# Two reorderings in a one-core streaming encoder step: the first unit's products in three passes, and the x updates of the output units ahead of two sums

## The chip, the cores and the metric

The kernel runs on one NeuronCore of a Trainium2 chip. The metric is the device time of one execution in microseconds (us); lower is better. Engines are TensorE (PE in the profile, with its weight loads as PEld), VectorE (DVE), ScalarE (ACT), GpSimd (POOL) and SyncE (SP), which here only issues DMAs.

## What is computed

A two-layer encoder with 512 prompt tokens and 32 sample tokens, taken together as 544 columns. Around each mixer stand two half-step FFNs, so there are four FFNs; the first is the first thing that runs:

```python
for layer in range(DEPTH):                       # DEPTH = 2
    x = x + 0.5 * swiglu(rms_norm(x, ffn1_norm[layer]), ffn1_w_in[layer], ffn1_w_out[layer])
    h = rms_norm(x, mix_norm[layer])
    ...                                          # attention + HGRN2 (even), gated DeltaNet (odd)
    x = x + o
    x = x + 0.5 * swiglu(rms_norm(x, ffn2_norm[layer]), ffn2_w_in[layer], ffn2_w_out[layer])
y = rms_norm(x, final_norm)
```

`swiglu(h, w_in, w_out)` is `(silu(gate) * up) @ w_out` with `gate, up = split(h @ w_in, 2)`. D_MODEL is 1024 and D_FF 2816, all in float32.

## The kernel before

**Layout.** `x` lies in SBUF as eight tiles of 128 features by 544 tokens. Each product in near-float32 precision is made of three products of a reduced type: the operand and the weight are each split into a high part (`xh`, `wh`: a ScalarE copy that rounds) and a low part (`xl`, `wl`: a VectorE subtraction), and TensorE sums high by high, high by low (of x) and low (of the weight) by high. The 544 tokens go in two matmuls, of 288 and 256 columns; such two matmuls are called a pair here. Two PSUM banks hold one output tile of 128 by 544.

**Norm.** The first product of an FFN takes x times gain, without the norm's factor. Beside it ScalarE squares the tiles (`sq`, L678), GpSimd adds the squares up in `ssq` (`feed_pool`, L686 to L696), TensorE sums over the partitions (`stats_pe`, L698), ScalarE takes the square root (`stats_act`, L705), VectorE the reciprocal (`stats_dve`, L709). The factor is multiplied in behind the product.

**Start.** SyncE issues the loads of `x_sample`, the first half of x's features (`xnat`, counted in `in_loaded`), the first unit's weights (`raw[0]`), the second half of x (`in2_loaded`), some small vectors, and then a stream of weights that waits for buffers. ScalarE issues `ident` and seven rows of gains, eight DMAs in `vec_loaded`. `load_pe` (L3217) waits for all eight, turns the gain rows into columns in bank 6 (L3221), then transposes the eight tiles of x through three slots of PSUM banks (L3233, L3234). `load_dve` (L3250) copies each into `x` and follows it with the low part of the tile before (`feed_dve`, L680); with tile 4 it makes the low part of the first weights (`split_lo`, L641, 128 by 2048). ScalarE makes the high part of a tile and its square in turn (`feed_act`, L670), with the high part of the weights (`split_hi`, L633) ahead of tile 4.

**First unit.** `ffn_whole_pe` (L786) waits for the low part of the weights, and for each of two output tiles c runs over the eight tiles k of x with three pairs each (`mm3`, L652). For the first FFN (`u.f == 0`) the statistics come behind c = 1, and then `late_pe` (L3237): it waits for the square root and transposes further small vectors (L3244 to L3248). Then comes the second unit (L782).

**Order.** Each engine has one program order written out by hand, and waits for others by counters (semaphores).

**Output units.** In each FFN, groups of two "seven" units (inputs' products, L852) alternate with one "mid" unit, 32 in all, eight for each FFN, which multiplies four tiles of the hidden layer by `w_out` and adds the result to x. A mid unit has four blocks on TensorE (`ffn_mid_pe`, L861), of twelve pairs each, which use two PSUM slots in turn: block m may start once the x update of block m - 2 is done. VectorE runs beside it (`ffn_mid_dve`, L1221): for the next seven unit v it makes four sums of weight blocks (`weight_sum_dve`, L991) and the low parts of what ScalarE has rounded (`op_split_lo`, L769), the low parts of the hidden layer (`hidden_lo`, L912) and the four x updates (`x_update`, L1170), of which the last stands in the unit behind.

Of the kernel before, what the change touches and what calls it, by code (L numbers as in the profile page):

```python
# [24 lines left out]
ACT = mybir.ActivationFunctionType  # L25
# [4 lines left out]
P = 128  # L30
D = 1024
KT = D // P
SEQ = 512
DEC = 32
T = SEQ + DEC
TOKENS = (slice(0, 288), slice(288, T))
PCOLS = (slice(224, 512), slice(0, T - 288))
# [115 lines left out]
def build(nc, ctx, io):  # L153
# [14 lines left out]
    def again(first, count):  # L168

        return Later(first.sem, first.credit + count)  # L170
# [374 lines left out]
    sm_packed = again(lam_exp, 1)  # L545
    tail_psum = again(an_wide, 4)
    tail_copied = again(an_hi, 4)
    tail_stored = again(in_loaded, 32)

    y_scaled = again(an_inv, 3)  # L550
    y_psum = again(an_psum, 1)
# [62 lines left out]
    def entry(op):  # L614
# [2 lines left out]
        flat = lambda w: w[e // 4][:].rearrange("p k n -> p (k n)")[:, (e % 4) * KH * P:(e % 4 + 1) * KH * P]  # L617
        block = lambda w: flat(w).rearrange("p (k n) -> p k n", n=P)
        return block(wh), block(wl)
    VECS, LATE = 8, 9  # L620

    def late_vectors(sp):
        sp.dma_start(rows_conv[0:4, :], io["conv_w"][0]).then_inc(late_loaded.sem, 16)
# [17 lines left out]
    def split_lo(dve, u, slot, kt=KT):  # L641

        dve.wait_ge(hi_done.sem, hi_done.at(u + 1))
        nc.vector.tensor_tensor(wl[slot][:, 0:kt, :], raw[slot][:, 0:kt, :], wh[slot][:, 0:kt, :].bitcast(F32),  # L644
                                ALU.subtract).then_inc(lo_done.sem, 1)
# [17 lines left out]
    def gain_of(n, m):  # L663
        return gain(n, m) if isinstance(m, int) else gain_at(n, m)

    def tile(buf, m):

        return buf[:, m, :] if isinstance(m, int) else buf[:, ds(m, 1), :].rearrange("p a t -> p (a t)")

    def feed_act(act, n, m, par, products=True):  # L670

        act.wait_ge(x_ready.sem, x_ready.at(8 * n + m + 1))
        set_apart(act)
        if products:
            nc.scalar.activation(tile(xh, m), tile(x, m), ACT.Copy, scale=gain_of(n, m)).then_inc(xh_ready.sem, 1)
        act.wait_ge(ssq_done.sem, ssq_done.at(8 * n + m - 1))
        set_apart(act)
        nc.scalar.activation(sq[par][:], tile(x, m), ACT.Square).then_inc(sq_ready.sem, 1)  # L678
# [35 lines left out]
    def slot_free(pe, n, slot):  # L714

        pe.wait_ge(x_ready.sem, x_ready.at(8 * n + 5 + slot))
# [52 lines left out]
    def op_split_lo(dve, u, i):  # L769
        op, nk = u.op + i, block_nk(u, i)  # L770
        hi, lo = entry(op)
        dve.wait_ge(op_hi.sem, op_hi.at(op + 1))
        nc.vector.tensor_tensor(lo[:, 0:nk, :], op_source(u, i), hi[:, 0:nk, :].bitcast(F32), ALU.subtract).then_inc(op_lo.sem, 1)  # L773

    def block3(pe_out, op, nk, rh, rl, rk, first, last):
# [7 lines left out]
                                           start=first and k == 0 and a == 0, stop=last and k == nk - 1 and a == 2)  # L783
        return ins

    def ffn_whole_pe(pe, u, n):  # L786
        c0 = U_FFN[u.f]
        pe.wait_ge(lo_done.sem, lo_done.at(c0 + 1))
        for c in range(2):
            if u.f:  # L790
                slot_free(pe, n, c)
            for k in range(KT):
                if c == 0:
                    pe.wait_ge(xl_ready.sem, xl_ready.at(8 * n + k + 1))
                last = mm3(c, 0, k, c, xh, xl, k, k == 0, k == KT - 1)
            last.then_inc((gate_psum if c == 0 else unit_done).sem, 1)
            if c == (1 if u.f == 0 else 0):
                stats_pe(pe, n)
                if u.f == 0:
                    late_pe(pe)  # L800

    def ffn_plain_pe(pe, u, n):
        f, j = u.f, u.pair
# [366 lines left out]
    def x_update(dve, u, c):  # L1170

        m = 4 * u.pair + c
        dve.wait_ge(op_used.sem, op_used.at(u.op + c + 1))
        if u.part:
            dve.wait_ge(x_part.sem, x_part.at(part_updates(u, m - 7)))
        nc.vector.scalar_tensor_tensor(out=two(x[:, m, :]), in0=halves(2 + c % 2), scalar=0.5, in1=two(x[:, m, :]),  # L1176
                                       op0=ALU.mult, op1=ALU.add).then_inc(x_part.sem, 1)
# [43 lines left out]
    def ffn_mid_dve(dve, u):  # L1221
        before, v = ffns[u.f][u.at - 1], ffns[u.f][u.at + 1]
        tail_dve(dve, before)
        weight_sum_dve(dve, v, 0)
        op_split_lo(dve, v, 0)
        weight_sum_dve(dve, v, 1)
        op_split_lo(dve, v, 1)
        weight_sum_dve(dve, v, 2)
        weight_sum_dve(dve, v, 3)
        hidden_lo(dve, before, 0, 1)  # L1230
        x_update(dve, u, 0)
        op_split_lo(dve, v, 2)
        hidden_lo(dve, before, 1, 2)
        op_split_lo(dve, v, 3)
        x_update(dve, u, 1)
        op_split_lo(dve, v, 4)
        op_split_lo(dve, v, 5)
        x_update(dve, u, 2)
        op_split_lo(dve, v, 6)
# [1976 lines left out]

    def load_pe(pe):  # L3217

        pe.wait_ge(vec_loaded.sem, vec_loaded.at(16 * VECS))
        for m in range(KT):  # L3220
            ins = nc.tensor.transpose(ps[:, 6, 7 * m:7 * m + 7], rows_gain[:, m * P:(m + 1) * P], ident[0:7, 0:7])  # L3221
        ins.then_inc(cols_psum.sem, 1)
        for m in range(KT):
            if m == 0:
                pe.wait_ge(in_loaded.sem, in_loaded.at(32))
            if m == 2:
                pe.wait_ge(cols_ready.sem, cols_ready.at(1))
            if m == KT // 2:
                pe.wait_ge(in2_loaded.sem, in2_loaded.at(16))
            pe.wait_ge(x_ready.sem, x_ready.at(m - 2))  # L3230
            s = 1 + m % 3
            for b in range(NB):
                nc.tensor.transpose(ps[:, 2 * s, b * P:(b + 1) * P], xnat[:, b, m * P:(m + 1) * P], ident[:])  # L3233
            nc.tensor.transpose(ps[:, 2 * s + 1, 0:DEC], xnat_dec[:, m * P:(m + 1) * P],  # L3234
                                ident[0:DEC, 0:DEC]).then_inc(xt_done.sem, 1)

    def late_pe(pe):  # L3237

        pe.wait_ge(late_loaded.sem, late_loaded.at(16 * LATE))
        pe.wait_ge(consts_set.sem, consts_set.at(1))  # L3240
        pe.wait_ge(rms_ready.sem, rms_ready.at(1))
        pe.wait_ge(cols_ready.sem, cols_ready.at(1))
        for m in range(24):
            nc.tensor.transpose(ps[:, 6, 7 * (KT + m):7 * (KT + m) + 7], rows_conv[:, m * P:(m + 1) * P], ident[0:7, 0:7])  # L3244
        for m in range(4):
            nc.tensor.transpose(ps[:, 6, LB + 2 * m:LB + 2 * m + 2], rows_lb[:, m * P:(m + 1) * P], ident[0:2, 0:2])
        nc.tensor.transpose(ps[:, 6, G3:G3 + 3], rows_g3[:], ident[0:3, 0:3]).then_inc(cols_psum.sem, 1)
        nc.tensor.matmul(ps[:, 7, 0:272], ones[0:1, :], row_lam[:], start=True, stop=True).then_inc(lam_psum.sem, 1)  # L3248

    def load_dve(dve):  # L3250
        dve.wait_ge(cols_psum.sem, cols_psum.at(1))
        nc.vector.tensor_copy(cols[:, 0:7 * KT], ps[:, 6, 0:7 * KT]).then_inc(cols_ready.sem, 1)
        nc.vector.tensor_copy(pick[0:32, :], ident[0:32, 0:16])
        nc.vector.tensor_copy(pick[32:48, :], ident[32:48, 32:48])
        for m in range(KT):
            dve.wait_ge(xt_done.sem, xt_done.at(m + 1))
            s = 1 + m % 3
            nc.vector.tensor_copy(x[:, m, 0:SEQ], ps[:, 2 * s, :])
            nc.vector.tensor_copy(x[:, m, SEQ:T], ps[:, 2 * s + 1, 0:DEC]).then_inc(x_ready.sem, 1)
            if m == KT // 2:  # L3260
                split_lo(dve, 0, 0)
            if m:
                if m == 1:
                    dve.wait_ge(cols_ready.sem, cols_ready.at(1))
                feed_dve(dve, 0, m - 1)
        feed_dve(dve, 0, KT - 1)

    def late_dve(dve):
        dve.wait_ge(cols_psum.sem, cols_psum.at(2))
# [98 lines left out]
    @block.scalar  # L3368
    def _(act):
        for s in (hi_done, tap0):  # L3370
            s.credit_by(act)

        act.dma_start(ident[:], io["c_ident"]).then_inc(vec_loaded.sem, 16)
        for l in range(2):
            for r, name in enumerate(("ffn1_norm", "mix_norm", "ffn2_norm")):
                act.dma_start(rows_gain[3 * l + r:3 * l + r + 1, :], io[name][l:l + 1, :]).then_inc(vec_loaded.sem, 16)
        act.dma_start(rows_gain[6:7, :], io["final_norm"].rearrange("(a n) -> a n", a=1)).then_inc(vec_loaded.sem, 16)
        act.wait_ge(cols_ready.sem, cols_ready.at(1))
        for m in range(KT):
            if m == KT // 2:  # L3380
                split_hi(act, 0, 0)
            feed_act(act, 0, m, m % 2)
        ffn_act(act, 0, 0, U_EVEN)
        even_proj_act(act, 1)
        hgrn_act(act)
        out_act(act, U_EVEN + 14, PLAIN_PARTS, 2, False)
        ffn_act(act, 1, 2, U_FFN[2])
        ffn_act(act, 2, 3, U_ODD)
        odd_act(act, 4)
        out_act(act, U_ODD + 16, PLAIN_PARTS, 5, False, True)  # L3390
        ffn_act(act, 3, 5)
        output_act(act, 6)
# [77 lines left out]
```

## Time and profile before

| | us |
|---|---|
| three runs | 2361.01, 2366.35, 2360.02 |
| their median | 2361.01 |
| the profiled execution | 2359.82 |
| its span | 2358.0 |

| engine | busy, us | share of the span |
|---|---|---|
| PE | 2311.9 | 98% |
| PEld | 2255.4 | 96% |
| DVE | 1646.2 | 70% |
| ACT | 1063.1 | 45% |
| POOL | 298.9 | 13% |

The span is what the profiler saw from first to last instruction; the device time of the same execution is 1.8 us more. Times in views are us from the span's start, those of single instructions may be in ns. Matmuls are pipelined, so two that follow each other overlap in the list; how far apart they start tells the pace. The profile's share of granted clock is 1 at the upper of TensorE's two levels (2.4 GHz) and 0.5 at the lower (1.2 GHz).

### The profile page before, as it was taken

How to read it: one execution, taken by the hardware profiler on the slowest of the kernel's cores; microseconds unless marked ns; L12 is line 12 of the kernel's file. 1: busy time of each engine (PE TensorE's matmuls, PEld its weight loads, DVE VectorE, ACT ScalarE, POOL GpSimd, SP SyncE). 2: the span in 40 equal slices, each digit the busy share in tenths (PEclk: the TensorE clock that was granted, in tenths of full speed). 3: DMA queues.
4: the chain of work that ended last, by engine and by line, in shares of the span. 5: the costliest groups of instructions: out<-in, count | busy, mean ns of one | idle time of the engine just before them, and what ended most of it. 6: DMA issues, size and time to landing. Idle time of an engine off the chain costs nothing.

```text
span 2358.0 us, 44517 instructions
## 1 busy us (share of the span) xinstructions
PE 2311.9 (98%) x18296; PEld 2255.4 (96%) x18296; DVE 1646.2 (70%) x2689; ACT 1063.1 (45%) x1951; POOL 298.9 (13%) x252
## 2 busy tenths in 40 slices
PE   7999999999999999999999999999999999999998
PEld 6999999988989999999999999999999899999998
DVE  6876776656575967776976676788655657877674
ACT  4544444233324544444544444455344544544443
POOL 2100002000051100001200000243033432100001
PEclk9999999999999999999999999999999999999999
DMA  3322323322202222322223222322200002232222
GB/s 118 103 90 90 99 94 116 98 85 80 70 10 90 90 90 91 108 90 90 90 90 106 92 90 90 101 72 90 77 27 1 10 28 90 90 107 91 90 91 73
DMA packets 174905, 194.70 MB, mean 83 GB/s; under 512 B 4810, under 2 KB 155726, under 8 KB 174697
## 3 DMA queue, kind: packets, MB, share of 16 engines
q1 hardware_dynamic: 161902, 181.64, 23.6%
q10 hardware_dynamic: 12162, 8.11, 1.2%
q8 instruction: 147, 2.41, 0.4%
q0 software_dynamic: 640, 2.10, 0.3%
q14 instruction: 54, 0.44, 0.1%
HBM read 185.73 MB, written 6.10 MB: 81 GB/s over the span
## 4 chain that ended last, share of the span: by engine, by line
PE 91%; DVE 5%; issue 1%; ACT 1%; POOL 0%; DMA 0%; ACTq 0%; DVEq 0%
PE ps L852 31%; PE ps L782 28%; PE ps L659 19%; PE ps L3061 2%; PE ps L3046 1%; PE ps L3192 1%; DVE wl L644 1%; PE ps L3034 1%; PE ps L1631 1%; PE ps L2099 0%; PE ps L2196 0%; DVE hl L916 0%; PE ps L1320 0%; DVE wl L773 0%; PE ps L3080 0%
## 5 line engine op out<-in xcount | busy, mean ns | idle before, releaser
L852 PE MATMUL ps<-bop,wh 128*128 128x272 f32 x4032 | 764.0, 289 | 0.0
L852 PEld LDWEIGHTS ps<-bop,wh 128*128 128x128 f32 x4032 | 633.6, 188 | 0.1
L852 PE MATMUL ps<-bop,wl 128*128 128x272 f32 x2016 | 583.6, 289 | 0.0
L773 DVE TENSOR_TENSOR wl<-raw,wh 128x512 fp32r<-128x512 f32 (+1 forms) x456 | 318.2, 710 | 279.3 <-ACT wh L767 274.8
L852 PEld LDWEIGHTS ps<-bop,wl 128*128 128x128 f32 x2016 | 379.1, 188 | 0.0
L767 ACT ACTIVATE wh<-raw 128x512 fp32r<-128x512 f32 (+1 forms) x456 | 264.8, 610 | 247.2 <-PE ps L782 209.8
L782 PE MATMUL ps<-hh,wh 128*128 128x288 f32 (+1 forms) x1408 | 290.4, 287 | 5.5 <-DVE x L1176 5.5
L782 PE MATMUL ps<-hl,wh 128*128 128x288 f32 (+1 forms) x1408 | 289.6, 287 | 0.0
L782 PE MATMUL ps<-hh,wl 128*128 128x288 f32 (+1 forms) x1408 | 288.7, 286 | 0.0
L659 PE MATMUL ps<-xh,wh 128*128 128x288 f32 x1088 | 232.7, 295 | 3.9 <-DVE wl L644 2.8
L782 PEld LDWEIGHTS ps<-hh,wh 128*128 128x128 f32 x1408 | 215.0, 188 | 11.4 <-issue 11.4
L659 PE MATMUL ps<-xl,wh 128*128 128x288 f32 x1088 | 224.5, 287 | 0.0
L659 PE MATMUL ps<-xh,wl 128*128 128x288 f32 x1088 | 223.7, 287 | 0.0
L782 PEld LDWEIGHTS ps<-hh,wl 128*128 128x128 f32 x1408 | 215.2, 188 | 0.0
L782 PEld LDWEIGHTS ps<-hl,wh 128*128 128x128 f32 x1408 | 214.7, 188 | 0.0
L767 ACT ACTIVATE wh<-wsum 128x512 fp32r<-128x512 f32 x256 | 159.6, 627 | 112.6 <-DVE wsum L998 86.6
L773 DVE TENSOR_TENSOR wl<-wsum,wh 128x512 fp32r<-128x512 f32 x256 | 175.1, 684 | 17.4 <-ACT wh L767 13.7
L659 PEld LDWEIGHTS ps<-xh,wh 128*128 128x128 f32 x1088 | 166.6, 189 | 16.2 <-issue 7.4
L692 POOL COPY ssq<-sq 128x544 f32<-128x544 f32 x7 | 5.2, 741 | 1307.4 <-ACT sq L678 1307.4
L659 PEld LDWEIGHTS ps<-xh,wl 128*128 128x128 f32 x1088 | 166.7, 188 | 0.0
L659 PEld LDWEIGHTS ps<-xl,wh 128*128 128x128 f32 x1088 | 166.4, 188 | 0.0
L644 DVE TENSOR_TENSOR wl<-raw,wh 128x2048 fp32r<-128x2048 f32 x41 | 94.5, 2304 | 38.7 <-ACT wh L639 38.7
(475 smaller groups left out, 3692.4 us busy)
## 6 DMA issues: line engine op xcount, KB each, us to landing
raw<-ffn_w_in SPq DMA_DIRECT2D x88, 1024.0 KB, 5.1
raw<-ffn_w_out SPq DMA_DIRECT2D x32, 1024.0 KB, 5.0
raw<-odd_w_in SPq DMA_DIRECT2D x16, 1024.0 KB, 5.8
raw<-even_w_in SPq DMA_DIRECT2D x14, 1024.0 KB, 5.0
raw<-ffn_w_out SPq DMA_DIRECT2D x16, 768.0 KB, 4.2
raw<-even_w_out SPq DMA_DIRECT2D x4, 1024.0 KB, 5.0
raw<-odd_w_out SPq DMA_DIRECT2D x4, 1024.0 KB, 5.2
xnat<-x_prompt SPq DMA_DIRECT2D x2, 1024.0 KB, 12.1
```

What stands on the lines that cost most here:

```text
L644: nc.vector.tensor_tensor(wl[slot][:, 0:kt, :], raw[slot][:, 0:kt, :], wh[slot][:, 0:kt, :].bitcast(F32), ALU.subtract).then_inc(lo_done.s ...
L659: ins = nc.tensor.matmul(ps[:, 2 * pe_out + b, PCOLS[b]], w, r[:, rk, TOKENS[b]], start=first and a == 0, stop=last and a == 2)
L692: nc.gpsimd.tensor_copy(ssq[:], sq[0][:]).then_inc(ssq_done.sem, 1)
L767: nc.scalar.activation(entry(op)[0][:, 0:block_nk(u, i), :], op_source(u, i), ACT.Copy).then_inc(op_hi.sem, 1)
L773: nc.vector.tensor_tensor(lo[:, 0:nk, :], op_source(u, i), hi[:, 0:nk, :].bitcast(F32), ALU.subtract).then_inc(op_lo.sem, 1)
L782: ins = nc.tensor.matmul(ps[:, 2 * pe_out + b, PCOLS[b]], w[:, k, :], r[:, rk + k, TOKENS[b]], start=first and k == 0 and a == 0, stop=las ...
L852: ins = nc.tensor.matmul(ps[:, bank, 0:TH], w[:, k, :], bop[:, r, k, :], start=i in S_OPEN and k == 0 and a == 0, stop=k == KH - 1 and a = ...
L1631: ins = nc.tensor.matmul(ps[:, 4 + m, 0:width(b)], att[64 * m:64 * m + 64, h, b * P:(b + 1) * P], att[64 * m:64 * m + 64, 4 + h, 0:width(b ...
L3034: ins = nc.tensor.transpose(bank(g, 2, n, n)[:, h, :], dX[g][0:n, h, 0:n], ident[0:n, 0:n])
L3046: ins = nc.tensor.matmul(bank(g, 0, n, n)[:, h, :], strict[0:n, h, 0:n], dX[g][0:n, h, 0:n], start=True, stop=True)
L3061: ins = nc.tensor.matmul(bank(g, 0, n, n)[:, h, :], dU[g][0:n, h, 0:n], dZ[g][0:n, h, 0:n], start=True, stop=True)
L3192: ins = nc.tensor.matmul(ps[:, 2 * (2 * q + c) + b, PCOLS[b]], w, r[:, k, TOKENS[b]], start=k == 0 and a == 0, stop=k == KT - 1 and a == 2)
```

## The change

In the first unit:

- TensorE runs all high by high products over both output tiles (for each tile of x, both c), then all high by low, then low by high, c = 0 and then c = 1. The passes wait for `hi_done`, `xl_ready` and `lo_done` in turn. The statistics stand behind c = 0 of the third pass, `late_pe` behind c = 1.
- `load_pe` starts on x when `ident` (now counted in `in_loaded`) and the first half of x are in, and transposes the gains after two tiles, into bank 0. The slots of the tiles are shifted by one.
- VectorE copies two tiles, then the gains, then for each tile m its copy and the low part of tile m - 2; the low part of the first weights comes last.
- ScalarE loads the gains of both layers with one DMA for each norm, runs a Square on a spare column ahead of its first wait, makes the high part of the weights ahead of tile 3, and squares only tiles 0 and 1 between the copies; the squares of tiles 2 to 7 come behind all copies.

In the output units (`ffn_mid_dve`) the x update of block 0 moves ahead of the third and fourth sum.

```diff
@@ feed_act
-    def feed_act(act, n, m, par, products=True):
+    def feed_act(act, n, m, par, products=True, squares=True):
...
+        if not squares:
+            return
         act.wait_ge(ssq_done.sem, ssq_done.at(8 * n + m - 1))
@@ first unit
+    def first_whole_pe(pe):
+        w_hi, w_lo = wh[0], wl[0]
+
+        def product(c, k, w, r, first, last):
+            for b in range(2):
+                ins = nc.tensor.matmul(ps[:, 2 * c + b, PCOLS[b]], w[:, k, c * P:(c + 1) * P], r[:, k, TOKENS[b]],
+                                       start=first, stop=last)
+            return ins
+
+        pe.wait_ge(hi_done.sem, hi_done.at(1))
+        for k in range(KT):
+            pe.wait_ge(xh_ready.sem, xh_ready.at(k + 1))
+            for c in range(2):
+                if k == 0 and c == 1:
+                    pe.wait_ge(x_ready.sem, x_ready.at(6))
+                product(c, k, w_hi, xh, k == 0, False)
+        for k in range(KT):
+            pe.wait_ge(xl_ready.sem, xl_ready.at(k + 1))
+            for c in range(2):
+                product(c, k, w_hi, xl, False, False)
+        pe.wait_ge(lo_done.sem, lo_done.at(1))
+        for c in range(2):
+            for k in range(KT):
+                last = product(c, k, w_lo, xh, False, k == KT - 1)
+            last.then_inc((gate_psum if c == 0 else unit_done).sem, 1)
+            if c == 0:
+                stats_pe(pe, 0)
+        late_pe(pe)
@@ ffn_mid_dve
         op_split_lo(dve, v, 1)
+        x_update(dve, u, 0)
         weight_sum_dve(dve, v, 2)
         weight_sum_dve(dve, v, 3)
         hidden_lo(dve, before, 0, 1)
-        x_update(dve, u, 0)
@@ load_pe
-        pe.wait_ge(vec_loaded.sem, vec_loaded.at(16 * VECS))
+        pe.wait_ge(in_loaded.sem, in_loaded.at(48))
         for m in range(KT):
-            ins = nc.tensor.transpose(ps[:, 6, 7 * m:7 * m + 7], rows_gain[:, m * P:(m + 1) * P], ident[0:7, 0:7])
-        ins.then_inc(cols_psum.sem, 1)
-        for m in range(KT):
-            if m == 0:
-                pe.wait_ge(in_loaded.sem, in_loaded.at(32))
             if m == 2:
-                pe.wait_ge(cols_ready.sem, cols_ready.at(1))
+                pe.wait_ge(vec_loaded.sem, vec_loaded.at(16 * VECS))
+                for g in range(KT):
+                    ins = nc.tensor.transpose(ps[:, 0, 7 * g:7 * g + 7], rows_gain[:, g * P:(g + 1) * P], ident[0:7, 0:7])
+                ins.then_inc(cols_psum.sem, 1)
...
-            s = 1 + m % 3
+            s = 1 + (m + 1) % 3
@@ load_dve
+        turned(0)
+        turned(1)
         dve.wait_ge(cols_psum.sem, cols_psum.at(1))
...
+        dve.wait_ge(cols_ready.sem, cols_ready.at(1))
+        for m in range(2, KT):
+            turned(m)
+            feed_dve(dve, 0, m - 2)
+        feed_dve(dve, 0, KT - 2)
         feed_dve(dve, 0, KT - 1)
+        split_lo(dve, 0, 0)
@@ scalar
-        act.dma_start(ident[:], io["c_ident"]).then_inc(vec_loaded.sem, 16)
-        for l in range(2):
-            for r, name in enumerate(("ffn1_norm", "mix_norm", "ffn2_norm")):
-                act.dma_start(rows_gain[3 * l + r:3 * l + r + 1, :], io[name][l:l + 1, :]).then_inc(vec_loaded.sem, 16)
+        act.dma_start(ident[:], io["c_ident"]).then_inc(in_loaded.sem, 16)
+        for r, name in enumerate(("ffn1_norm", "mix_norm", "ffn2_norm")):
+            act.dma_start(rows_gain[r:r + 4:3, :], io[name]).then_inc(vec_loaded.sem, 16)
...
+        act.wait_ge(consts_set.sem, consts_set.at(1))
+        nc.scalar.activation(lamv[:, 7:8], eps[:, 0:1], ACT.Square)
         act.wait_ge(cols_ready.sem, cols_ready.at(1))
         for m in range(KT):
-            if m == KT // 2:
+            if m == 3:
                 split_hi(act, 0, 0)
-            feed_act(act, 0, m, m % 2)
+            feed_act(act, 0, m, m % 2, squares=m < 2)
+        for m in range(2, KT):
+            feed_act(act, 0, m, m % 2, products=False)
```

## Rows read from the trace of the kernel before

**Rows 1.** Waits of TensorE: us in total, times, longest us.
```profile
PE ps L3221 <- DMA rows_gain<-final_norm: 8.3, 1, 8.3
PE ps L782 <- DVE x L1176: 5.5, 4, 1.4
PE ps L659 <- DVE wl L644: 3.5, 2, 2.8
```

**Rows 2.** Chain of waits, 0 to 80 us: start us, us, what.
```profile
30.76 6.99 PE ps L659 x54
...
42.16 37.48 PE ps L782 x288
```

**Rows 3.** Timeline of TensorE, start: start us, us, engine, line, instruction [idle before].
```profile
9.26 1.11 PE L3233 MATMUL ps<-ident,xnat 128*128 128x128 f32 x4
...
14.40 1.11 PE L3233 MATMUL ps<-ident,xnat 128*128 128x128 f32 x4
...
18.42 1.11 PE L3233 MATMUL ps<-ident,xnat 128*128 128x128 f32 x4
...
22.58 0.82 PE L659 MATMUL ps<-xh,wh 128*128 128x288 f32 x2 [2.81 <-DVE wl L644]
...
25.46 0.48 PE L659 MATMUL ps<-xh,wh 128*128 128x288 f32 x2
...
37.59 1.08 PE L702 MATMUL ps<-ssq,ones 128*128 128x288 f32 x4
39.67 1.61 PE L3244 MATMUL ps<-ident,rows_conv 7*128 7x7 f32 x24 [1.01 <-ACT ssq L707]
...
42.09 0.52 PE L782 MATMUL ps<-xh,wh 128*128 128x288 f32 x2
```

**Rows 4.** Issue of x's second half, and its time to landing.
```profile
2.20 0.61 SPq L3354 DMA_DIRECT2D xnat<-x_prompt  x1
...
DMA to landing us min/median/max: 12.1/12.1/12.1
```

**Rows 5.** Timeline of GpSimd: three adds of squares, at the start and the end.
```profile
21.26 2.47 POOL L696 TENSOR_TENSOR ssq<-ssq,sq 128x544 f32<-128x544 f32 x1 [0.89 <-ACT sq L678]
...
28.50 1.62 POOL L696 TENSOR_TENSOR ssq<-ssq,sq 128x544 f32<-128x544 f32 x1 [0.18 <-POOL ssq L696]
...
2336.00 1.36 POOL L696 TENSOR_TENSOR ssq<-ssq,sq 128x544 f32<-128x544 f32 x1 [2.60 <-ACT sq L678]
```

**Rows 6.** Timeline of VectorE and ScalarE at the start.
```profile
19.83 2.69 DVE L644 TENSOR_TENSOR wl<-raw,wh 128x2048 fp32r<-128x2048 f32 x1 [1.47 <-ACT wh L639]
...
26.33 0.77 DVE L682 SCALAR_TENSOR_TENSOR xl<-x,cols,xh 128x544 fp32r<-128x544 f32 x1
...
27.72 2.98 DVE L682 SCALAR_TENSOR_TENSOR xl<-x,cols,xh 128x544 fp32r<-128x544 f32 x2
27.91 0.75 ACT L675 ACTIVATE xh<-x,cols 128x544 fp32r<-128x544 f32 x1
...
30.62 3.65 DVE L773 TENSOR_TENSOR wl<-raw,wh 128x512 fp32r<-128x512 f32 x4
```

**Rows 7.** Busy time of each engine in one us; the third number from the end is the granted clock.
```profile
43.00:44.00 1.00, 1.00 (x6) 1.00 (x6) 0.97 (x3) 0.20 (x1) 0.00 (x0) 0.50 0.00 0
```

**Rows 8.** Timelines of the first output unit, and of the second.
```profile
105.61 0.68 DVE L1004 TENSOR_TENSOR wsum<-raw,wsum 128x512 f32<-128x512 f32 x1
...
107.45 0.72 DVE L1176 SCALAR_TENSOR_TENSOR x<-ps,x 128x544 f32<-128x544 f32 x1
...
108.31 0.49 PE L782 MATMUL ps<-hh,wh 128*128 128x288 f32 x2 [1.37 <-DVE x L1176]
...
109.92 0.72 DVE L1176 SCALAR_TENSOR_TENSOR x<-ps,x 128x544 f32<-128x544 f32 x1
...
138.28 0.41 PE L782 MATMUL ps<-hh,wl 128*128 128x288 f32 x2
...
138.96 0.68 DVE L1004 TENSOR_TENSOR wsum<-raw,wsum 128x512 f32<-128x512 f32 x1
...
139.67 1.24 ACT L767 ACTIVATE wh<-wsum 128x512 fp32r<-128x512 f32 x2 [0.15 <-DVE wsum L1004]
```

More of the change, by code:

```diff
@@ L547, in build @@
     tail_copied = again(an_hi, 4)
-    tail_stored = again(in_loaded, 32)
+    tail_stored = again(in_loaded, 48)
     y_scaled = again(an_inv, 3)
@@ L619, in entry @@
         return block(wh), block(wl)
-    VECS, LATE = 8, 9
+    VECS, LATE = 4, 9
     def late_vectors(sp):
@@ L784, in block3 @@
         return ins
+    def first_whole_pe(pe):
[24 more added lines that the diff above has]
+        late_pe(pe)
     def ffn_whole_pe(pe, u, n):
+        if u.f == 0:
+            first_whole_pe(pe)
+            return
         c0 = U_FFN[u.f]
@@ L789, in ffn_whole_pe @@
         for c in range(2):
-            if u.f:
-                slot_free(pe, n, c)
+            slot_free(pe, n, c)
             for k in range(KT):
@@ L796, in ffn_whole_pe @@
             last.then_inc((gate_psum if c == 0 else unit_done).sem, 1)
-            if c == (1 if u.f == 0 else 0):
+            if c == 0:
                 stats_pe(pe, n)
-                if u.f == 0:
-                    late_pe(pe)
     def ffn_plain_pe(pe, u, n):
@@ L3250, in load_dve, with turned @@
     def load_dve(dve):
+        def turned(m):
+            dve.wait_ge(xt_done.sem, xt_done.at(m + 1))
+            s = 1 + (m + 1) % 3
+            nc.vector.tensor_copy(x[:, m, 0:SEQ], ps[:, 2 * s, :])
+            nc.vector.tensor_copy(x[:, m, SEQ:T], ps[:, 2 * s + 1, 0:DEC]).then_inc(x_ready.sem, 1)
+        turned(0)
+        turned(1)
         dve.wait_ge(cols_psum.sem, cols_psum.at(1))
-        nc.vector.tensor_copy(cols[:, 0:7 * KT], ps[:, 6, 0:7 * KT]).then_inc(cols_ready.sem, 1)
+        nc.vector.tensor_copy(cols[:, 0:7 * KT], ps[:, 0, 0:7 * KT]).then_inc(cols_ready.sem, 1)
         nc.vector.tensor_copy(pick[0:32, :], ident[0:32, 0:16])
         nc.vector.tensor_copy(pick[32:48, :], ident[32:48, 32:48])
[L3255 to L3259, printed above, removed]
-            if m == KT // 2:
[L3261 to L3265, printed above, removed]
+        dve.wait_ge(cols_ready.sem, cols_ready.at(1))
[3 more added lines that the diff above has]
+        feed_dve(dve, 0, KT - 2)
         feed_dve(dve, 0, KT - 1)
+        split_lo(dve, 0, 0)
     def late_dve(dve):
@@ L3371, in _ @@
             s.credit_by(act)
-        act.dma_start(ident[:], io["c_ident"]).then_inc(vec_loaded.sem, 16)
-        for l in range(2):
-            for r, name in enumerate(("ffn1_norm", "mix_norm", "ffn2_norm")):
-                act.dma_start(rows_gain[3 * l + r:3 * l + r + 1, :], io[name][l:l + 1, :]).then_inc(vec_loaded.sem, 16)
+        act.dma_start(ident[:], io["c_ident"]).then_inc(in_loaded.sem, 16)
+        for r, name in enumerate(("ffn1_norm", "mix_norm", "ffn2_norm")):
+            act.dma_start(rows_gain[r:r + 4:3, :], io[name]).then_inc(vec_loaded.sem, 16)
         act.dma_start(rows_gain[6:7, :], io["final_norm"].rearrange("(a n) -> a n", a=1)).then_inc(vec_loaded.sem, 16)
+        act.wait_ge(consts_set.sem, consts_set.at(1))
+        nc.scalar.activation(lamv[:, 7:8], eps[:, 0:1], ACT.Square)
         act.wait_ge(cols_ready.sem, cols_ready.at(1))
         for m in range(KT):
-            if m == KT // 2:
+            if m == 3:
                 split_hi(act, 0, 0)
-            feed_act(act, 0, m, m % 2)
+            feed_act(act, 0, m, m % 2, squares=m < 2)
+        for m in range(2, KT):
+            feed_act(act, 0, m, m % 2, products=False)
         ffn_act(act, 0, 0, U_EVEN)
```

## The prediction

> **What bounds the kernel now.** I read the list of TensorE's waits first. It is short: 8.3 us for the first loads, 5.5 us in four waits for an x update of VectorE, 3.5 us for the low part of the first weights [rows 1]. The chain of waits then says that from 42.16 us on TensorE runs 288 products without a gap up to 79.64 [rows 2]. So the kernel is bound by the count of TensorE's products, and only what lets TensorE begin earlier, or takes one of those waits away, can move the end. The change works at two such places: the first 42 us, and the four waits of 1.4 us.
>
> In the timeline of the start the reader is to see four stretches [rows 3]: eight tiles of x transposed from 9.26 to 19.7 (1.28 us a tile), 2.8 us of waiting for the low weights, 48 pairs of products from 22.58 to 37.59, and then statistics, a wait for the square root and 29 tiny transposes until 42.09, where the second unit begins. I price TensorE's work from here: 27 pairs from 30.76 [rows 2] to 37.59 [rows 3] are 0.25 us a pair at the upper clock level; the first six pairs took 2.9 us (22.58 to 25.46), 0.45 us for most.
>
> **The change part by part, at the start.**
>
> Loads. The second half of x is issued at 2.20 us and lands 12.1 us later, at 14.3 [rows 4]; the fifth tile was transposed at 14.40 [rows 3], so in the kernel before that landing was just met. The change doesn't touch SyncE's queue. ScalarE issues three gain loads in place of six; whatever that saves, and the earlier start of the first tiles (they no longer stand behind the gain loads, at least 8.3 us before), ends at the same landing. I take no gain from it. The cover is thin on the other side: two tiles, eight gain transposes (about 1 us) and two more tiles are 6.1 us, so the first half of x must be in by 8.2 us. The trace shows only that it was in by 9.26. If it lands then, TensorE ends its transposes 1.1 us late; I keep this for the range. So TensorE is through with its transposes at 14.35 + 4 x 1.29 = 19.5 us.
>
> First products. They now need only the high parts of weights and x, and begin at 19.55 in place of 22.58. Nothing of before shows dense products right behind transposes. The transposes did not bring the quick pace before: the six pairs behind them were slow. I take the same 2.9 us for the first six pairs. Of the 48 pairs 40 stand ahead of the statistics: 2.9 + 34 x 0.25 = 11.4, so TensorE comes to the statistics at 30.95.
>
> VectorE. It now turns two tiles before the gains, and the 2.7 us split of the low weights [rows 6] goes behind all tiles. A copy and a low part take 1.39 us a tile (26.33 to 27.72) [rows 6]; the last tile is transposed at 19.5, VectorE is then busy with the fifth low part until 20.2, copies the last tile until 20.9, and is done with the low parts at 23.1 to 24 and with the weights at about 26. The third pass wants them at 28.9. So both waits, of 2.8 us and 1.1 us, go at no price; what is queued behind the split is only the second unit. The reload of that weight buffer starts some 3.5 us later than before, but is read only behind the first square root; were this cover gone, it would cost 1 us for 1 us.
>
> ScalarE and GpSimd. Six of eight squares go behind all copies. This is what is late next. The last copy ends at 20.9 + 0.75 = 21.65 [rows 6], the third square at 22.3, and GpSimd then has six adds left, where before only three lay behind 26.7. The trace has three prices [rows 5]: 1.36 us where VectorE leaves it alone, 1.62 beside low parts, 2.47 where the split of 128x2048 lies beside it; 0.18 between two. I place them: one beside the last low parts (1.62), one beside the split (2.47), three alone (1.36 each, VectorE has nothing to do from 26 to 30.4), one beside the next unit's splits (1.62). That is 9.8 + 0.9 = 10.7 us, and the sum of squares is ready at 33.0. TensorE has waited 2 us for it.
>
> Statistics and late transposes. Statistics 1.0 us (37.59 to 38.68 before) until 34.0. The other half of the third pass, eight pairs, 2.0 us, lies beside the square root, which had cost TensorE 1.0 us of waiting. Late transposes 2.4 us as before (39.67 to 42.09). The second unit begins at 34.0 + 2.0 + 2.4 = 38.4 in place of 42.09: **3.7 us**. VectorE's reciprocal comes earlier by 4.7 us (square root ready at 34.7 in place of 39.4), so its chain into the next units moves by more than TensorE's, and the gap-free run of rows 2 stays one.
>
> Bounds of this term: six adds alone are 9.1 us, ready at 31.4, TensorE 5.3 us earlier; six adds at 2.47 are 15.7 us, ready at 38.0, TensorE 1.3 us later than before. I take the placement above, since each price there has a row with the same neighbour.
>
> Clock. From 43 to 44 us the granted clock is 0.50, the lower level of 1.2 GHz [rows 7]; it holds for about seven pairs at 0.45 in place of 0.25, 1.4 us. It fell after TensorE had done, since 38.68, only a wait and small transposes, 3.4 us. In the changed kernel the longest such stretches are the wait of 2 us and, 3 us of dense work later, the 2.4 us of transposes. I take it that the clock doesn't fall: **1.4 us**; the ends are 0 and 1.4, and something like the loss of 1.4 could come in the 2 us wait instead.
>
> **The change part by part, output units.** There are 32 (eight for each FFN). In the first of each FFN TensorE's third product block waits for the x update of block 0: that update starts at 107.45, TensorE at 108.31 after 1.37 us [rows 8]. Two sums of 0.6 us and one low part stand ahead of it. Moved, it starts at 105.61, where the first of the sums stood, and ends at 106.3, before TensorE asks (106.94). But the fourth block waits for the update of block 1, and that one keeps its place: it starts at 109.92 and ends at 110.6, as all that stands ahead of it is only reordered, and VectorE has no idle time there. TensorE, now through with the third block at 110.0, waits 0.7 us for it. So of 1.37 us 0.67 stays: x 4 = **2.7 us**. The ends are 0 (VectorE shifted by as much) and 5.5.
>
> In the other 28 units the update comes to stand where the sum now starts, at 138.96 in the unit of 135.53; the last pair of the block that it needs starts at 138.28 and takes 0.41 [rows 8]. So it waits for nothing, with 0.3 us in hand. The sums come 0.65 us later; ScalarE's copies of them are taken up by the unit after, several us away. I cost it at nothing; what it costs without that cover is the slower rival.
>
> **Sum.** 3.7 + 1.4 + 2.7 = 7.8 us. The profiled execution took 2359.8 us (span 2358.0 and 1.8 around it), 1.2 less than the median of the runs, 2361.0; the four times have their middle at about 2360.3. I go from there: 2352.5 us.
>
> **The rivals.**
>
> The clock falls all the same (in the wait ahead of the statistics or behind the late transposes): 6.4 us, 2353.9. For: such a wait is new. Against: neither stretch is as long as the one that preceded the fall.
>
> GpSimd starves. Here six adds meet low parts, the long split and the next four splits. For: the add beside the long split took 2.47 us, and most of the excess over 1.36 is the 1.24 us in which that split still ran [rows 5, 6]. If every such VectorE instruction stops GpSimd outright, the adds' 9.1 us and VectorE's 0.7 + 2.3 + 4 x 0.6 go one after the other: 14.5 us, ready at 36.8, the second unit at 42.2, nothing won at the start. Left is 2.7: 2357.6. Against: beside short instructions it was VectorE that was stretched (two low parts in 2.98 us, four splits in 3.65 [rows 6]), GpSimd only from 1.36 to 1.62. The Trainium skill (GPSIMD Engine Reference, 1. Specifications) says that GpSimd shares its SBUF interfaces with VectorE, with contention for VectorE instructions with two SBUF inputs; by that rule, taken as exclusion, this rival is the outcome, and the trace bears it out only in part.
>
> GpSimd is hardly stretched, sum ready at 31.4 to 31.9: 5.0 + 1.4 + 2.7 = 9.1, 2351.2. For: VectorE is idle through most of it.
>
> Slower. In the 28 regular output units the moved update has 0.3 us in hand. If VectorE waits there, or the delay of 0.65 us of two sums reaches TensorE through ScalarE's copies, it is paid 28 times: up to 18 us, less the 7.8 of the rest, 2370.7. It decides from the point at which the sums' copies have under 0.65 us in hand before their products. Against: ScalarE has copied both sums by 140.9 [rows 8], and their products stand in the unit after, which begins 12 us behind the start of this one at 135.53.
>
> The waits for x updates aren't what holds the output units (the place of VectorE as a whole is): 5.1 us, 2355.2.
>
> **How the numbers follow.** Forecast 0.46, clock falls 0.21, starved 0.11, hardly stretched 0.13, update worth nothing 0.05, slower 0.03, first half of x late (2353.5) within the forecast; 0.01 for the rest. Range: from the free GpSimd with some room, 2350.0, to the starved one, 2357.6. About 0.3% (7 us, below 2353.9 where the runs' median is 2361.0) is what a measurement of this kernel can tell from no change. The forecast lies on the near side of it by 1.4 us only: 0.8 of it counts as faster, a third of the clock rival, all of the free GpSimd: 0.55. Slower 0.03. Within 0.42.
>
> **What would show it.** Right: first products at 19.5 without a wait for the low weights; a TensorE wait of about 2 us for the sum of squares near 31 to 33; none for the square root; second unit at 38.4; no 0.50 in the clock near 40; in each FFN's first output unit no wait at the third block and one of 0.7 us at the fourth. Wrong: the sum of squares ready before 31 or after 35, products at the slow pace for longer than 3 us, a wait at other output units, or a total that moved by more than the start and the four waits did.

## The result, and the profile after

| | before | changed |
|---|---|---|
| median of six runs, us | 2360.2 | 2350.15 |
| lowest to highest, us | 2359.75 to 2366.35 | 2345.86 to 2351.15 |
| profiled execution, us | 2359.82 | 2350.17 |
| its span, us | 2358.0 | 2348.4 |

The medians differ by 10.1 us, where 7.8 were forecast in the sum. The ratio on record is 0.9949 (95% interval 0.9938 to 0.9959); it isn't the quotient of the two medians, which is 0.9957 and lies inside that interval, and the same holds for the ratios of the experiments below. The change is faster by more than 0.3%, but the time stands at the very low end of the range (2350.0 to 2357.6), and by the ratio, 2348.2, just under it. The total hides that both halves of the sum were wrong, in opposite directions.

First the waits of TensorE in the changed kernel (us in total, times, longest us), to set against [rows 1]. The change shifted line numbers: the x update is L1207, the transposes of x are L3262 and L3263, the statistics L704.

```profile
PE ps L3262 <- DMA xnat<-x_prompt: 7.4, 2, 6.3
PE ps L784 <- DVE x L1207: 3.5, 4, 0.9
...
PE ps L704 <- POOL ssq L698: 2.5, 1, 2.5
```

The waits for low weights are gone but for 0.7 us elsewhere; four waits for an x update are left, 0.9 us each in place of 1.4; and there is a new one of 2.5 us for GpSimd's sum of squares. The timeline of TensorE's start, to set against [rows 3]:

```profile
6.26 1.11 PE L3262 MATMUL ps<-ident,xnat 128*128 128x128 f32 x4 [6.26 <-DMA xnat<-x_prompt]
...
13.38 1.12 PE L3262 MATMUL ps<-ident,xnat 128*128 128x128 f32 x4 [1.09 <-DMA xnat<-x_prompt]
...
18.53 6.17 PE L793 MATMUL ps<-xh,wh 128*128 128x288 f32 x32
24.54 4.18 PE L793 MATMUL ps<-xl,wh 128*128 128x288 f32 x32
28.55 2.17 PE L793 MATMUL ps<-xh,wl 128*128 128x288 f32 x16
33.20 2.18 PE L704 MATMUL ps<-ssq,ones 128*128 128x288 f32 x4 [2.47 <-POOL ssq L698]
34.82 3.11 PE L793 MATMUL ps<-xh,wl 128*128 128x288 f32 x16
37.86 1.64 PE L3273 MATMUL ps<-ident,rows_conv 7*128 7x7 f32 x24
...
40.68 0.82 PE L784 MATMUL ps<-xh,wh 128*128 128x288 f32 x2
```

Read the starts. The first products begin at 18.53 (22.58 before), TensorE is at the statistics at 30.6, waits to 33.20, and then takes 1.6 us for the statistics and 3.0 for eight pairs, which took 1.0 and 2.0 in the working of the prediction. The second unit begins at 40.68: 1.4 us earlier, not 3.7. The granted clock shows why. These are stretches of the changed kernel: length, then busy us of PE, PEld, DVE, ACT, POOL with instructions, and the third number from the end is the clock.

```profile
32.50:36.50 4.00, 3.30 (x10) 2.84 (x11) 2.73 (x4) 2.24 (x3) 0.65 (x1) 0.57 0.05 14
36.50:39.50 3.00, 3.00 (x39) 2.85 (x37) 3.00 (x1) 1.47 (x3) 0.00 (x0) 1.00 0.98 333
39.50:47.00 7.50, 7.50 (x37) 6.80 (x36) 7.40 (x12) 4.70 (x7) 3.14 (x2) 0.54 0.01 4
```

TensorE ran at the lower level (1.2 GHz) in two stretches, from 33.0 to 36.5 and from 39.9 to 46.7; before there was one, 3.4 us long (42.7 to 46.1, of which [rows 7] shows one us). By 79.2 us, where the fifth unit begins, only 0.2 us of the start's gain is left (79.47 before, 79.23 after, by the timelines). At the first output unit it is 0.4 us (100.81 and 100.41).

So the 10 us come from the output units. Timelines of the second one (a regular unit), first in the kernel before, with the x update of block 0 on VectorE (L1176), then in the changed kernel:

```profile
135.53 0.42 PE L782 MATMUL ps<-hh,wh 128*128 128x288 f32 x2
...
140.80 0.71 DVE L1176 SCALAR_TENSOR_TENSOR x<-ps,x 128x544 f32<-128x544 f32 x1
...
141.25 0.41 PE L782 MATMUL ps<-hh,wl 128*128 128x288 f32 x2
141.66 0.49 PE L782 MATMUL ps<-hh,wh 128*128 128x288 f32 x2
141.98 0.41 PE L782 MATMUL ps<-hl,wh 128*128 128x288 f32 x2
...
147.70 0.41 PE L852 MATMUL ps<-bop,wh 128*128 128x272 f32 x2
```

```profile
134.63 0.42 PE L784 MATMUL ps<-hh,wh 128*128 128x288 f32 x2
...
140.35 0.41 PE L784 MATMUL ps<-hh,wl 128*128 128x288 f32 x2
140.60 0.40 PE L784 MATMUL ps<-hh,wh 128*128 128x288 f32 x2
...
146.54 0.41 PE L883 MATMUL ps<-bop,wh 128*128 128x272 f32 x2
```

Before, the unit ran from 135.53 to 147.70, 12.17 us; after, from 134.63 to 146.54, 11.91. Between the second and third block the pairs start 0.41 us apart in place of 0.25 (141.25 to 141.66), and the next start comes 0.32 later. The x update ends at 141.51, just as TensorE wants its buffer. That is a stall of a quarter of a microsecond, on none of the lines of the list of TensorE's waits. The traces have it in each of the 28 regular units: all are 12.16 or 12.17 us long before and 11.91 or 11.92 after, 7 us in all. The only sign of it in the lists is in that of the weight loads. These are the waits of TensorE's weight loads in the kernel before, from 120 to 400 us, the stretch with the seven regular units of the first FFN:

```profile
PEld ps L782 <- issue: 1.3, 7, 0.2
```

Seven times 0.2, put down to "issue". In the changed kernel the list of that stretch is empty.

### The profile page after: what moved, and what is told of

Its sections match the earlier page's. It is cut to its first block, busy times and chain, and to the rows that moved or that the text cites. A ratio compares the mean times of both kernels' runs of the same rounds, so it can differ in the third digit from the quotient of the medians.

```text
span 2348.4 us, 44520 instructions
## 1 busy us (share of the span) xinstructions
PE 2307.8 (98%) x18296; PEld 2256.6 (96%) x18296; DVE 1644.0 (70%) x2689; ACT 1063.7 (45%) x1952; POOL 299.8 (13%) x252
## 4 chain that ended last, share of the span: by engine, by line
PE 91%; DVE 6%; issue 1%; ACT 1%; POOL 1%; DMA 0%; DVEq 0%; SPq 0%; ACTq 0%; POOLq 0%
PE ps L883 31%; PE ps L784 27%; PE ps L659 19%; PE ps L3092 2%; PE ps L3077 1%; PE ps L3223 1%; PE ps L3065 1%; DVE wl L775 1%; PE ps L1662 1%; DVE wl L644 0%; POOL ssq L698 0%; DVE hl L947 0%; PE ps L2130 0%; PE ps L2227 0%; PE ps L1351 0%
## 5 line engine op out<-in xcount | busy, mean ns | idle before, releaser
L659 PE MATMUL ps<-xh,wh 128*128 128x288 f32 (+1 forms) x1056 | 225.3, 294 | 0.0
L659 PE MATMUL ps<-xl,wh 128*128 128x288 f32 (+1 forms) x1056 | 217.4, 287 | 0.0
L659 PE MATMUL ps<-xh,wl 128*128 128x288 f32 (+1 forms) x1056 | 216.7, 286 | 0.0
L659 PEld LDWEIGHTS ps<-xh,wh 128*128 128x128 f32 x1056 | 161.1, 188 | 11.7 <-issue 7.4
L659 PEld LDWEIGHTS ps<-xh,wl 128*128 128x128 f32 x1056 | 161.4, 188 | 0.0
L659 PEld LDWEIGHTS ps<-xl,wh 128*128 128x128 f32 x1056 | 161.1, 188 | 0.0
## 6 DMA issues: line engine op xcount, KB each, us to landing
xnat<-x_prompt SPq DMA_DIRECT2D x2, 1024.0 KB, 11.1
```

What stands on the lines that cost most here:

```text
L659: ins = nc.tensor.matmul(ps[:, 2 * pe_out + b, PCOLS[b]], w, r[:, rk, TOKENS[b]], start=first and a == 0, stop=last and a == 2)
```

## The experiments

All times are medians; the kernel before ran beside each of two groups. Its median was 2360.36 beside the kernels with the output units alone, the start alone, the squares between the copies and the statistics behind, and 2359.92 beside the other four. The changed kernel's 2350.15 is that of the first table.

**Which half brought the time.** The output units alone:

```diff
         op_split_lo(dve, v, 1)
+        x_update(dve, u, 0)
         weight_sum_dve(dve, v, 2)
         weight_sum_dve(dve, v, 3)
         hidden_lo(dve, before, 0, 1)
-        x_update(dve, u, 0)
```

> The kernel before with only the x update of block 0 moved ahead of the two sums in the 32 output units. Theory A (from the two traces: each of the 28 regular units was 0.25 us longer before, 12.16 against 11.91 us, since the update of block 0 ended at the moment at which TensorE wanted it; the four first ones 0.5 us): 28 x 0.25 + 4 x 0.5 = 9.0 us, 2351.2 against 2360.2, and 32 output units as long as in the changed kernel. Theory B (my prediction: only the four waits count, the regular units hide the update): 2 to 2.7 us, 2357.5 to 2358.2.

Measured 2351.67 (ratio 0.9957, 0.9945 to 0.9969): 8.7 us, where theory A had 9.0. Theory A holds. The second output unit runs from 135.30 to 147.21, 11.91 us; four waits of 0.9 remain. Next, the start alone:

```diff
@@ the changed kernel, ffn_mid_dve
-        x_update(dve, u, 0)
         weight_sum_dve(dve, v, 2)
         weight_sum_dve(dve, v, 3)
         hidden_lo(dve, before, 0, 1)
+        x_update(dve, u, 0)
```

> The changed kernel with the x update put back behind the sums, so only the start is changed. Theory A (what the start won was given back by a lower clock level, first in the 2.5 us wait for the sum of squares and again behind the late transposes): 0.3 to 1 us faster than before, 2359.2 to 2359.9, with two stretches of granted clock 0.5 before 50 us. Theory B (the start is worth the 5.1 us forecast and the output units the rest): 2355.

Measured 2357.66 in eleven runs, 2355.67 to 2359.59 (ratio 0.9987, 0.9978 to 0.9995): 2.7 us, more than A said and about half of B. The profiled execution was the slowest of them, 2359.59. In it the wait for the sum of squares was 3.2 us, the clock was at 0.50 from 33.1 to 39.9 and again from 43.3 to 46.8, and the first output unit begins when it did before. So the start is worth something between 0.8 and 4.7 us from one execution to the next. That the clock makes this difference is likely, not shown: only one execution has a trace, but the mean granted clock of the whole execution was 0.998 in four of the five quickest and 0.996 or 0.997 in the six others. The two halves add up to 11.4, the changed kernel shows 10.1.

**Is it lateness, or the order?** The update was moved by one place only:

```diff
@@ the kernel before, ffn_mid_dve
         weight_sum_dve(dve, v, 2)
         weight_sum_dve(dve, v, 3)
-        hidden_lo(dve, before, 0, 1)
         x_update(dve, u, 0)
+        hidden_lo(dve, before, 0, 1)
```

> The kernel before with the x update of block 0 moved ahead of one low part of the hidden layer only, so it stays behind both sums: 0.64 us earlier in place of 1.84. Theory A (in the regular units the update missed TensorE's need by 0.25 us, so any move of more than that wins the whole): 9 us, as for the full move, 2351.4; regular units 11.91 us. Theory B (what the regular units won came from the sums being out of the way of it, in proportion to the move): a third, 3 us, 2357.3.

Measured 2350.63 (0.9962, 0.995 to 0.9975), 9.3 us, as much as the full move. Regular units are 11.91 us long (134.97 to 146.88), and the first one of each FFN is 13.02 to 13.04, as with the full move. The waits of TensorE left in this kernel:

```profile
PE ps L782 <- DVE x L1176: 2.9, 4, 0.7
```

In the first output units these are waits at the third block (107.62 us), where the full move left them at the fourth. The move of one place was enough; theory A holds, and the update didn't have to go ahead of the two sums. The regular stall was an update that ended as it was wanted.

**What the first output units still wait for.** On top of the changed kernel, the update of block 1 was moved:

```diff
         op_split_lo(dve, v, 2)
+        x_update(dve, u, 1)
         hidden_lo(dve, before, 1, 2)
         op_split_lo(dve, v, 3)
-        x_update(dve, u, 1)
```

> The changed kernel with the x update of block 1 moved two places ahead as well (before the second low part of the hidden layer and one low part of the weights). If that update is what TensorE waits 0.87 us for in each first output unit: 4 x 0.87 = 3.5 us, 2346.7, with no wait at the fourth block. If VectorE as a whole is late there, the wait goes on to the next product that needs a low part, and the time stays at 2350.2.

Measured 2344.32 (0.9935, 0.9922 to 0.9947), 5.8 us below the changed kernel, where 3.5 were expected. The waits for x updates are gone, and the first output unit lasts 11.92 us in place of 13.04, 4 x 1.12 = 4.5 us. The rest, 1.3 us, is within the spread of its runs (2342.67 to 2348.29); in the profiled execution the start was as much ahead, with the second unit at 39.37 in place of 40.68. That execution was the slowest of the five: from the first to the last of the transposes of L2593, in a later stage, it took 140.1 us (1778.6 to 1918.7) against 136.0 in the changed kernel (1783.4 to 1919.4), 2.4 of these 4.1 us in waits for VectorE that are longer than in the changed kernel. The edit touches nothing there, and the cause is not known. VectorE as a whole wasn't late: nothing took the wait's place.

**What gives the start's gain back.** First the cause of the late sum. GpSimd in the changed kernel:

```profile
21.44 3.82 POOL L698 TENSOR_TENSOR ssq<-ssq,sq 128x544 f32<-128x544 f32 x1 [7.15 <-ACT sq L680]
25.44 1.36 POOL L698 TENSOR_TENSOR ssq<-ssq,sq 128x544 f32<-128x544 f32 x1 [0.18 <-POOL ssq L698]
...
31.58 1.56 POOL L698 TENSOR_TENSOR ssq<-ssq,sq 128x544 f32<-128x544 f32 x1 [0.18 <-POOL ssq L698]
```

The sum is ready at 33.1. VectorE's work beside the long add, and beside the last one:

```profile
19.68 2.17 DVE L684 SCALAR_TENSOR_TENSOR xl<-x,cols,xh 128x544 fp32r<-128x544 f32 x3
21.76 2.28 DVE L644 TENSOR_TENSOR wl<-raw,wh 128x2048 fp32r<-128x2048 f32 x1
31.21 3.68 DVE L775 TENSOR_TENSOR wl<-raw,wh 128x512 fp32r<-128x512 f32 x4 [7.17 <-ACT wh L769]
```

In the next kernel all squares stand between the copies again:

```diff
-            feed_act(act, 0, m, m % 2, squares=m < 2)
-        for m in range(2, KT):
-            feed_act(act, 0, m, m % 2, products=False)
+            feed_act(act, 0, m, m % 2)
```

> The changed kernel with all eight squares between ScalarE's copies, as before; the rest of the change stays. If the late squares are what makes the sum of squares late: GpSimd's sum is ready by 27 us in place of 33.2, TensorE meets the statistics at about 30.7 without a wait, the clock doesn't fall there, the second unit begins at 36 in place of 40.7, and the time is 2345.5, or down to 2343 if the clock doesn't fall behind the late transposes either. If VectorE's low parts, slower beside GpSimd, become the bound of the three passes instead, TensorE waits there and the time stays within 1 us of 2350.2.

Measured 2344.92 (0.9931, 0.992 to 0.9943), 5.2 us below the changed kernel. Its GpSimd and TensorE:

```profile
24.03 1.63 POOL L698 TENSOR_TENSOR ssq<-ssq,sq 128x544 f32<-128x544 f32 x1 [0.18 <-POOL ssq L698]
```

```profile
28.57 2.20 PE L793 MATMUL ps<-xh,wl 128*128 128x288 f32 x16
30.61 1.08 PE L704 MATMUL ps<-ssq,ones 128*128 128x288 f32 x4
...
36.08 0.58 PE L784 MATMUL ps<-xh,wh 128*128 128x288 f32 x2
```

The sum is ready at 25.7, TensorE doesn't wait, the second unit begins at 36.08, and the clock falls once, at 36.4, behind the late transposes. The three passes did not suffer: high by high begins at 18.60, the statistics at 30.61. So it was the late squares, not the passes, that the start paid for. Against the kernel with the output units alone (2351.67) this start is worth 6.8 us.

Next, the clock alone. The wait was filled with products that nothing reads:

```diff
@@ first_whole_pe, ahead of stats_pe
+                for i in range(10):
+                    for b in range(2):
+                        nc.tensor.matmul(ps[:, 6 + b, PCOLS[b]], w_lo[:, i % KT, 0:P], xh[:, i % KT, TOKENS[b]], start=True, stop=True)
```

> The changed kernel with ten pairs of products more (2.5 us; into the banks that the statistics overwrite, so nothing is read of them) in TensorE's wait for the sum of squares. Theory A (the wait without products is what brings the clock down at 33): granted clock 1 at 33 to 36.5, statistics and the last eight pairs at the upper level, 1.6 to 2 us faster than the changed kernel although TensorE does more: 2348.2 to 2348.6, and 2346.8 if the fall behind the late transposes gets shorter too. Theory B (the clock falls in any case, or the fall costs nothing since VectorE's reciprocal is the bound behind it): 2350 or more.

Measured 2347.23 (0.9945, 0.9932 to 0.9957): 2.9 us below the changed kernel, for more work. From 32.5 to 36.5 us:

```profile
32.50:36.50 4.00, 4.00 (x29) 3.66 (x29) 3.73 (x4) 2.30 (x3) 0.75 (x1) 1.00 0.07 9
```

The clock stays up, the second unit begins at 38.87 in place of 40.68, and the later fall is 3.4 us long in place of 6.8. The statistics begin at 33.32, against 33.20, so the added products cost nothing. That is theory A, and between the medians the clock cost the changed kernel 2.9 us. But the fall doesn't follow from the wait with certainty. The same stretch in the kernel with the second update moved, which had the wait of 3.3 us:

```profile
32.50:36.50 4.00, 3.04 (x20) 2.81 (x20) 3.73 (x4) 2.51 (x3) 0.90 (x1) 1.00 0.04 6
```

Here the clock held through a longer wait, and was down from 38.6 to 45.4 instead. These are single executions: where the clock falls differs from one to the next, and I can't say from them how often.

Last, the order of the statistics:

```diff
             last.then_inc((gate_psum if c == 0 else unit_done).sem, 1)
-            if c == 0:
-                stats_pe(pe, 0)
+        stats_pe(pe, 0)
         late_pe(pe)
```

> The changed kernel with the statistics behind both output tiles of the third pass, as before the change. TensorE then comes to the statistics at about 32.7, the sum is ready at 33.2: a wait of 0.5 us in place of 2.5, no fall of the clock at 33; but the wait of 1 us for the square root is back. Second unit at 37.5 in place of 40.7. If the clock fell because of the 2.5 us wait: 2345.5 to 2347. If the order of the statistics is worth what I took it for (1 us) and the clock falls in any case: 2351.

Measured 2348.39 (0.9947, 0.9934 to 0.9959; six runs from 2344.74 to 2353.84). TensorE in the profiled execution, one of the two quickest (2345.11):

```profile
33.53 1.18 PE L704 MATMUL ps<-ssq,ones 128*128 128x288 f32 x4 [1.62 <-POOL ssq L698]
35.72 1.62 PE L3272 MATMUL ps<-ident,rows_conv 7*128 7x7 f32 x24 [1.01 <-ACT ssq L709]
...
38.17 0.82 PE L784 MATMUL ps<-xh,wh 128*128 128x288 f32 x2
```

Part of this was expected: no fall at 33, the wait for the square root back, the second unit at 38.17, 0.7 later than expected. The wait for the sum was 1.6 us, not 0.5: the first pass was 0.8 us shorter here (18.51 to 23.71), and the sum was ready 0.3 later. The median lies between the two theories. The mean granted clock was 0.997 or 0.998 in the three quicker runs and 0.996 in the three slower ones, so the clock differs here too, and with this spread the runs don't decide how much this order alone is worth.

**Together.** Squares between the copies and the second update moved, both on the changed kernel:

```diff
-            feed_act(act, 0, m, m % 2, squares=m < 2)
-        for m in range(2, KT):
-            feed_act(act, 0, m, m % 2, products=False)
+            feed_act(act, 0, m, m % 2)
...
         op_split_lo(dve, v, 2)
+        x_update(dve, u, 1)
         hidden_lo(dve, before, 1, 2)
         op_split_lo(dve, v, 3)
-        x_update(dve, u, 1)
```

> The changed kernel with the squares between the copies (as in e3_squares_between) and the x update of block 1 two places ahead (as in e6_second_update). The two places don't touch each other: 2344.9 less 3.5, 2341.4. If one eats up the other: not below 2343.

Measured 2340.64 (0.9915, 0.9901 to 0.9928): 19.3 us below the kernel before, 9.5 below the changed one, and the gains add up (4.3 us on top of the squares alone). Of all kernels here it is the fastest.

## Why the prediction was right or wrong

**The 28 regular output units, costed at nothing: wrong, 7.0 us, the largest error.** The step that failed is "So it waits for nothing, with 0.3 us in hand" and, resting on it, "I cost it at nothing". The step asked whether VectorE would have to wait in the new place. It didn't ask whether TensorE was waiting in the old one, and it was, for 0.25 us in each unit. The numbers were there: the update started at 140.80 and takes 0.7, TensorE wants it 24 pairs after 135.53, at 141.5. My 0.25 us a pair, times 48, gives a unit of 12.0 by the same working, and 12.17 was measured. I read the list of waits as complete, and it is not: the list shows a pair as 0.41 us long where the next begins after 0.25, so a start that is 0.16 late leaves no idle time to be seen.

**The four first units: mechanism right, size off.** The third block's wait went, a wait at the fourth came. The wait measured 0.87 us, not 0.7, and the unit got 0.50 us shorter (13.54 to 13.04), not 0.67: 2.0 us where 2.7 stood.

```profile
109.52 0.72 DVE L1207 SCALAR_TENSOR_TENSOR x<-ps,x 128x544 f32<-128x544 f32 x1
110.38 0.49 PE L784 MATMUL ps<-hh,wh 128*128 128x288 f32 x2 [0.87 <-DVE x L1207]
```

The sum had TensorE go on where the update ends. It goes on 0.14 us later, here (110.24 to 110.38) and before (108.17 to 108.31 [rows 8]); this is nearly all of the difference. Moving the second update, which took the wait away and left 11.92 us, shows the mechanism.

**The start's 3.7 us: the working held up to the statistics, and failed behind them.** The prediction has the earlier loads end "at the same landing", with no gain. But the second half of x landed 11.1 us after its issue, not 12.1, so the products began 1.0 us earlier than forecast. This is not one execution's luck: the profiles of kernels with the old start have 12.0 or 12.1, those with the new one 11.1 to 11.5. Why it lands earlier no run shows. The first half was in by 6.26, so the fear of a late one was empty. The slow pace behind the transposes held for longer than the 2.9 us that I took from before: 16 pairs took 6.0 us, not 5.4. (The view gives 1.00 for the granted clock of these stretches, 22.5 to 25.5 before and 18.5 to 24.5 after, although the first pairs of each go 0.45 us apart, as they do where it gives 0.50; here only the pace shows it.) TensorE was at the statistics at 30.6 (30.95 forecast). GpSimd's sum was ready at 33.1 (33.0 forecast), and that it fits is partly luck: the first two adds took 3.82 and 1.36 where I had placed 1.62 and 2.47, 1.1 us more, and they began 0.9 earlier. So GpSimd did starve in one place, but only there: three low parts and the long split lay back to back from 19.7 to 24.0, and 2.6 us of that beside the add. The Trainium skill (GPSIMD Engine Reference, 1. Specifications) has contention with VectorE instructions that have two SBUF inputs; that one add, 2.5 us longer than alone, agrees with GpSimd being shut out. Beside the short splits it was VectorE that was stretched (four in 3.68 us), and the add took 1.56. What failed behind the sum is the clock: the second unit began 2.3 us later than forecast (40.68 against 38.4), 0.2 by the start of the statistics and 2.1 by the slower pace of all that follows it.

**The clock: the step that failed is "I take it that the clock doesn't fall", and its rival was priced too low.** Its reason was that no stretch was as long as the 3.4 us ahead of the old fall. The kernel with the squares between the copies refutes this: no wait, dense products from 31.34 to 33.63, 2.45 us of late transposes, and the clock fell at 36.4. It fell during or behind the late transposes in all ten profiles, between 36.4 and 43.7 us. The rival allowed one fall of 1.4 us. In the changed kernel there were two: the one in the wait made the statistics and eight pairs 1.6 us longer, the one behind the late transposes made these 0.4 longer and lasted for 13 pairs in place of seven, and the filled wait gives 2.9 us for the first with what follows from it. For the wait the runs show no rule: with 2.5 us of it the clock fell, with 3.3 in another kernel it held. Why stays open.

**The sum.** Forecast 3.7 + 1.4 + 2.7 + 0 = 7.8. The profiles of before and after give 0.4 + 2.0 + 7.0 = 9.4 of the 9.65 that they differ by; the runs of the halves give 2.7 and 8.7. The start's 5.1 (3.7 + 1.4) was too much by two to five, the units' 2.7 too little by six: that the total came near is luck, by two errors that partly cancel. "Faster by over 0.3%" came true for a reason that was not in the cases.

**The rivals.** The clock's fall came, larger. GpSimd was neither starved throughout (36.8 for the sum) nor hardly stretched (31.4 to 31.9). The rival that takes the waits for x updates to be worth nothing (2355.2) was wrong in the other direction. The slower one, that the delay of two sums reaches TensorE, left no sign: no regular unit is longer than its 48 pairs (11.91 us).

## What to carry to other kernels

Before costing a moved step at nothing, measure the stage it stands in against its bare work, here 48 pairs by the pace inside a block, and ask of each repeated stage where the difference lies: a quarter of a microsecond that no list of waits names is worth 7 us in 28 places. When an update frees a buffer, look at when it ends against when the buffer is wanted, and move it by one place first. When dense work is pulled ahead on TensorE, pull what feeds the next stage on the other engines as well: a new wait costs its length and, in some executions, a stretch at the lower clock level behind it.

## What the runs showed of the hardware that was not expected

- A wait of TensorE doesn't tell by its length whether the clock falls: in the changed kernel the clock was at the lower level twice within 14 us (33.0 to 36.5, at the end of a wait of 2.5 us, and 39.9 to 46.7), with the filled wait once, for 3.4 us, and in the kernel with the second update moved it held through a wait of 3.3 us and was down from 38.6 to 45.4. Around the late transposes it fell in all ten profiles.
- Transposes for 12 us (6.26 to 18.5, with 1.1 us of waiting in it) left TensorE at the slow pace at its first dense products: high by high took 6.0 us for 16 pairs, high by low 4.0.
- An add of GpSimd took 1.36 us with VectorE idle and 3.82 us when its first 2.6 us lay beside VectorE instructions with two SBUF inputs that followed each other without a gap (a low part, then the split of 2.28 us): about the time alone plus the time beside them. With the squares between the copies it took 1.63 beside low parts, and there VectorE's were stretched (three in 4.79 us, in place of 2.17).
